# Expert blocks of two half blocks, each with its own expert, in the MoE loop of a two-layer backbone

## What is computed

```python
scores = jax.nn.sigmoid((h @ router_w).astype(jnp.float32))
...
_, idx = lax.top_k(jnp.where(expert_mask, biased, -jnp.inf), TOP_K)     # 8 of 64
...
# assignments sorted by expert, each expert's rows padded to blocks
def run_block(args):
    tok, wt, e = args
    xb = h[tok]
    hid = jax.nn.silu(xb @ w_gate[e]) * (xb @ w_up[e])                  # 1024 -> 256
    return (hid @ w_down[e]) * wt[:, None]                              # 256 -> 1024
```

## Time and profile before

| | |
|---|---|
| time, median of 3 runs | 2135.89 us (2134.73 to 2139.37) |
| the profiled execution | 2138.5 us, its span from first to last instruction 2136.7 us |
| mean granted TensorE clock | 0.948 of full speed |
| busy: TensorE matmul, weight load | 1835.1 us (86%), 992.2 us |
| busy: VectorE, ScalarE, GpSimd | 846.2, 542.0, 426.2 us |
| `up` (L1208) | 5120 matmuls, 643.0 us busy |
| `down` (L1221) | 1264 matmuls, 306.5 us busy |
| expert weights | 384 transfers of 1 MB |
| moved by DMA | 578.28 MB |

### The profile page before, as it was taken

How to read it: one execution, slowest core, us unless ns; L and a number is a source line. 1 busy time by engine, 2 the same in 40 slices (tenths; PEclk the granted TensorE clock), 3 DMA queues, 4 the chain that set the end, 5 groups by cost and what they waited for, 6 DMA issues and landing times. The chain is left out here.

```text
span 2136.7 us, 39465 instructions
## 1 busy us (share of the span) xinstructions
PE 1835.1 (86%) x11495; PEld 992.2 (46%) x11496; DVE 846.2 (40%) x2836; ACT 542.0 (25%) x1163; POOL 426.2 (20%) x417
## 2 busy tenths in 40 slices
PE   4999699879999999999997589879688887888885
PEld 3545454435445545445553355545444444444442
DVE  2245563363333333333334526543532323223334
ACT  2142352222222222222221214233222222222221
POOL 0001300012223223222321000130122222222220
PEclk8999899999999999999999889969799999999998
DMA  8315510449999789897985853631599999999994
GB/s 278 126 66 201 188 60 1 177 170 377 369 388 357 257 309 359 315 376 270 383 334 198 297 158 110 250 129 34 209 354 370 409 399 411 397 406 400 363 385 185
DMA packets 170400, 578.28 MB, mean 271 GB/s; under 512 B 29756, under 2 KB 34592, under 8 KB 153448
## 3 DMA queue, kind: packets, MB, share of 16 engines
q1 hardware_dynamic: 134592, 515.49, 62.7%
q0 software_dynamic: 29056, 60.07, 7.7%
q10 hardware_dynamic: 6696, 1.98, 0.4%
HBM read 565.73 MB, written 45.75 MB: 286 GB/s over the span
## 5 line engine op out<-in xcount | busy, mean ns | idle before, releaser
L1208 PE MATMUL bank<-arena 128*64 128x256 f32 x5120 | 643.0, 395 | 124.8 <-DMA arena<-in_exp_w_down 81.5
L1208 PEld LDWEIGHTS bank<-arena 128*64 128x64 f32 x5120 | 353.0, 140 | 293.1 <-DMA arena<-in_exp_w_down 86.8
L676 POOL DMA_INDIRECT yrows<-arena x158 | 160.3, 1014 | 832.8 <-ACT arena L907 814.7
L1221 PE MATMUL bank<-arena 128*64 128x512 f32 x1264 | 306.5, 606 | 0.7 <-issue 0.5
L657 POOL DMA_INDIRECT arena<-hrows,arena x164 | 185.9, 1133 | 144.3 <-DVE arena L1650 91.6
L1680 DVE TENSOR_TENSOR arena<-arena,bank 64x256 f32<-64x256 f32 x160 | 68.0, 425 | 353.9 <-ACT arena L891 353.8
L902 ACT ACTIVATE arena<-bank 128x128 f32<-128x128 f32 x158 | 44.2, 280 | 565.6 <-PE bank L1227 565.6
L907 ACT ACTIVATE arena<-bank 128x512 f32<-128x512 f32 x158 | 94.4, 597 | 210.1 <-PE bank L1221 210.1
L973 PE MATMUL bank<-arena 128*128 128x512 f32 (+3 forms) x384 | 133.9, 512 | 11.7 <-DVE arena L1337 11.7
L1645 DVE COPY arena<-bank 128x3 f32<-128x3 f32 x164 | 26.4, 161 | 288.9 <-PE bank L1192 288.3
L1199 PE MATMUL bank<-arena 128*128 128x128 f32 x648 | 121.9, 311 | 7.8 <-DMA arena<-hrows,arena 7.8
(11 more groups left out here) (297 smaller groups left out, 1834.1 us busy)
## 6 DMA issues: line engine op xcount, KB each, us to landing
arena<-in_exp_w_gate SPq DMA_DIRECT2D x128, 1024.0 KB, 8.8
arena<-in_exp_w_up SPq DMA_DIRECT2D x128, 1024.0 KB, 11.1
arena<-in_exp_w_down SPq DMA_DIRECT2D x128, 1024.0 KB, 9.0
arena<-in_w_ada SPq DMA_DIRECT2D x10, 3072.0 KB, 13.7
arena<-yrows SPq DMA_DIRECT2D x24, 1024.0 KB, 16.3
arena<-in_w_ada SPq DMA_DIRECT2D x8, 2048.0 KB, 9.9
arena<-in_w_in SPq DMA_DIRECT2D x8, 2048.0 KB, 18.8
arena<-in_w_out SPq DMA_DIRECT2D x4, 2048.0 KB, 12.1
```

The costliest lines, as they stand in the source:

```text
L676: pool.indirect_dma_start(out=yrows, out_offset=bass.IndirectOffsetOnAxis(ap=SIXS[u], axis=0), in_=YSB[u], in_offset=None, bounds_check=2 ...
L1208: ins = pe.matmul(bank[b_par][64 * gu:64 * gu + 64, 0:HID], XGT[b_par][:, c, hh, :], wv[:, gu, hh, c, :], start=(c8 == 0), stop=(c8 == 7))
L1221: ins = pe.matmul(bank[2 + b_par][64 * cg:64 * cg + 64, :], HIDT[b_par][:, c, :], wv[:, c, cg * 512:(cg + 1) * 512], start=(c == 0), stop= ...
```

## The change

A block still has 64 slots, but they are two units of 32, each with its own expert. VectorE counts in units (every expert has at least one), and the table holds a unit's expert. `up` and `down` run on four column groups of 32 columns instead of two of 64: gate and up, times two units; two halves of the output, times two units. So each has twice as many matmuls of the same 256 or 512 moving columns. The ring has four slots, the fourth in the region of `H`; the waits for gate and up on one side and for down on the other are separate. `pe.If` now picks by the slot of the first unit (four) and by whether the second unit has the same expert (two), eight copies of each piece of code. `one_hot` copies the two experts' columns of `KV` to a fixed place (`KVP`), so `meta` looks nothing up.

```diff
-MAXB = (T * TOPK + NE * (SLOTS - 1)) // SLOTS
-TABN = 144
+MAXU = (T * TOPK + NE * (UNIT - 1)) // UNIT + 2
+MAXB = MAXU // 2
+TABN = 208
+NSLOT = 4
...
-        ring = [rRING + 6144 * k for k in range(3)]
+        ring = [rRING + 6144 * k for k in range(3)] + [rH]
...
+                    units_up_to = sp.value_load(TABP[0:1, bass.ds(i * NSLOT + u, 1)], min_val=0, max_val=MAXU)
+                    used = sp.snap((units_up_to + 1) // 2)
+                    sp.wait_ge(sp_land[u], i * 32 + (base_land[u] + 32))
+                    sp.wait_ge(sp_dn[u], i * 16 + 16)
...
+                for e in (0, 1, 3, 2):
+                    if e < 3:
+                        sp.wait_ge(*done_of[P_OUT + e])
+                    else:
+                        sp.wait_ge(pe_sh, 4)
+                        sp.wait_ge(pool_hr, 16 * NTS)
                     load_up(e, e)
                     load_down(e, e)
...
                     for t in TS:
-                        ins = pe.matmul(bank[7][:, 0:3], OH[b_par][:, t, :], KV[:, t, bass.ds(e, 1), :].rearrange("p a c -> p (a c)"),
-                                        start=(t == T0), stop=(t == NT - 1))
+                        for un in range(2):
+                            ins = pe.matmul(bank[7][SLOTS * un:SLOTS * un + SLOTS, 0:3], OH[b_par][:, t, un, :], KVP[b_par][:, t, 3 * un:3 * un + 3],
+                                            start=(t == T0), stop=(t == NT - 1))
...
                         for gu in range(2):
-                            ins = pe.matmul(bank[b_par][64 * gu:64 * gu + 64, 0:HID], XGT[b_par][:, c, hh, :], wv[:, gu, hh, c, :],
-                                            start=(c8 == 0), stop=(c8 == 7))
+                            for un in range(2):
+                                r = 64 * gu + UNIT * un
+                                ins = pe.matmul(bank[b_par][r:r + UNIT, 0:HID], XGT[b_par][:, c, un, hh, :], wv[un][:, gu, hh, c, :],
+                                                start=(c8 == 0), stop=(c8 == 7))
...
+                def experts_of(b):
+
+                    e = expert_of(b * 2)
+                    e2 = expert_of(b * 2 + 1)
+                    return e, pe.snap(e % NSLOT), pe.snap(e2 - e)
+
+                def in_slots(slot, step, body):
+
+                    def pair(k):
+                        with pe.If(step == 0):
+                            body((k, k))
+                        with pe.Else():
+                            body((k, (k + 1) % NSLOT))
+
+                    with pe.If(slot == 0):
+                        pair(0)
+                    with pe.Else():
+                        with pe.If(slot == 1):
+                            pair(1)
+                        with pe.Else():
+                            with pe.If(slot == 2):
+                                pair(2)
+                            with pe.Else():
+                                pair(3)
...
-                        meta(1 - u, b + 3, b + 4, b + 3)
-                        slot_now = None if u == 0 else slot
-                        e = expert_of(b + 1)
-                        slot = pe.snap(e % 3)
+                        meta(1 - u, b + 4, b + 3)
+                        now = None if u == 0 else (e, slot, step)
+                        e, slot, step = experts_of(b + 1)
                         pe.wait_ge(a_xe, b + 2)
...
                         turn_tokens(u, i * 16 + 32)
                         if u == 0:
-                            slot_now = pe.snap(expert_of(b) % 3)
+                            now = experts_of(b)
                         pe.wait_ge(a_h, b + 1)
                         pe.wait_ge(a_y, b + 1)
...
-                for m in range(1, NTOK // SLOTS):
-                    link(dve.scalar_tensor_tensor(out=NB, in0=CNT, scalar=float(m * SLOTS), in1=NB, op0=ALU.is_gt, op1=ALU.add))
+                for m in range(1, NTOK // UNIT):
+                    link(dve.scalar_tensor_tensor(out=NB, in0=CNT, scalar=float(m * UNIT), in1=NB, op0=ALU.is_gt, op1=ALU.add))
+                link(dve.tensor_scalar(NB, NB, 1.0, None, ALU.max))
...
                 def one_hot(par, b, chain):
 
-                    e = expert_of(b)
+                    es = [expert_of(b * 2 + un) for un in range(2)]
                     if not (isinstance(b, int) and b == 0):
                         dve.wait_ge(v_oh, b)
-                    chain(dve.tensor_scalar(RR[:, T0:].unsqueeze(2), GG[:, T0:, bass.ds(e, 1)], BASE[:, 0:1], None, ALU.subtract))
+                    for un in range(2):
+                        dve.tensor_copy(KVP[par][:, T0:, 3 * un:3 * un + 3], KV[:, T0:, bass.ds(es[un], 1), :].rearrange("p t a c -> p t (a c)"))
+                        ins = dve.tensor_scalar(RR[:, T0:, un:un + 1], GG[:, T0:, bass.ds(es[un], 1)], BASE[:, 0:1], None, ALU.subtract)
+                    chain(ins)
```

More of the change, by code:

```diff
@@ L235, in build @@
         NBH = at(o, 1); o += 1
-        RR = at(o, 4); o += 4
+        RR = at(o, NT, 2); o += 8
+        KVP = [at16(o + 12 * k, NT, 6) for k in range(2)]; o += 24
+        EB2 = at(o, 2); o += 2
         BASE = at(o, 1); o += 1
@@ L416, in landed @@
             return sp_land[k], 16 * sum(d for m, d in enumerate(dmas_of[:n + 1]) if slot_of(m) == k)
[L418 removed]
+        base_land = [16 * sum(d for m, d in enumerate(dmas_of) if slot_of(m) == k) for k in range(NSLOT)]
         with nc.Block() as block:
@@ L1200, in turn_tokens, with up @@
                     ins.then_inc(pe_x, 1)
-                def up(b_par, k, chunks, last):
-                    wv = at(ring[k], 2, 2, 4, HID)
+                def up(b_par, ks, chunks, last):
+                    wv = [at(ring[k], 2, 2, 4, HID) for k in ks]
                     for c8 in chunks:
@@ new lines, in down_landed, with down @@
+                def down_landed(e, ks):
+                    k, k2 = ks
+                    pe.wait_ge(sp_dn[k], e * 4 + (16 - 4 * k))
+                    if k2 != k:
+                        pe.wait_ge(sp_dn[k2], e * 4 + (20 - 4 * k2))
+                def down(b_par, ks):
+                    wv = [at(ring[k] + 4096, 2, DM) for k in ks]
+                    for c in range(2):
+                        for un in range(2):
+                            for cg in range(2):
+                                r = 64 * un + UNIT * cg
+                                ins = pe.matmul(bank[2 + b_par][r:r + UNIT, :], HIDT[b_par][:, c, UNIT * un:UNIT * un + UNIT],
+                                                wv[un][:, c, cg * 512:(cg + 1) * 512], start=(c == 0), stop=(c == 1))
+                    ins.then_inc(pe_dn, 1)
@@ L1234, in _, with first_up @@
                 turn_tokens(0, 16)
-                meta(0, 2, 3, 2)
+                meta(0, 3, 2)
                 turn_tokens(1, 16)
-                e = expert_of(0)
+                _, _, step = experts_of(0)
                 pe.wait_ge(a_xe, 1)
-                for k in range(3):
-                    with pe.If(e % 3 == k):
-                        expert_landed(e, k)
-                        up(0, k, range(8), True)
+                def first_up(ks):
+                    up_landed(0, ks)
+                    up(0, ks, range(8), True)
+                with pe.If(step == 0):
+                    first_up((0, 0))
+                with pe.Else():
+                    first_up((0, 1))
                 with pe.Fori(0, pairs) as i:
```

120 lines of the change are left out of this document (55 added, 65 removed).

## The result

The changed kernel takes 3977.05 us (median of 4 runs, 3962.26 to 3983.86) beside 2136.37 us of before on the same chip: ratio 1.862, 95% interval 1.857 to 1.866. The profiled execution has a span of 3975.4 us, 1838.7 more than before's 2136.7. The forecast of 3601 us had the sign, the place and the mechanism; it was 376 us short.

A forecast was written before the change was run, and what follows sets the result against it. Before, TensorE paced layer 0 and the weight stream layer 1; changed, reloaded code was to bound both. 2138.5 plus 1005 (layer 0), 458 (layer 1) and 4 gave 3605.5, in terms of the median 3601 us; range 2040 to 4400.

The forecast's parts named there:

- Blocks and array: Expert loops: 80 and 48 blocks; four column groups run side by side, so array time per block stays 4.1, 0.7, 1.9 us.
- sequencer: TensorE's instruction handling, lookups and branches: a pass of two blocks takes 17.9 us in layer 0, even 9.5, odd 8.4.
- Rival 1: All code pieces stay; the sequencer's pass decides layer 0, +31 us: 2173 us (2115 to 2230); chance 0.26.
- Rival 2: Faster: pieces stay and the sequencer keeps up, deciding from 8.4 us a block downwards; about 2050 us; chance 0.12.
- Rival 3: Four groups don't overlap with weights of 32 columns: 14.3 us a block, 2730 us; chance 0.07.
- The store: TensorE's instruction memory: holds at least 4 pieces, upper size unknown; the changed loop's 11.4 pieces likelier don't fit.
- Entries a pass: Expert loops on TensorE: a pass enters, and so loads again, about ten of the body's 11.4 code pieces.
- Price of an entry: Loading a code piece: between 1.5 and 5.9 us, middle 3.7, less 1.3 hidden, so 2.4 us each.
- The parts outside the loops: VectorE's longer tables and one-hots before the loops, +13 us, less 9 for the expert loaded early: +4.
- The weights: Fourth slot and separate `w_down` semaphore load one more expert early: 8.5 us off layer 1's stream, nothing in layer 0.

The follow-up runs named there:

- the run whose code stays: The changed kernel with both halves of a block taking the first expert's weights (one slot's weights), halving the code copies: 2152.0 us beside 2150.8, ratio 1.0004.

## Why the prediction was right, and where it was short

**Blocks and array: right; sequencer: right in the sum.** 80 and 48 blocks; 4.11 us for `up` with its transposes (forecast 4.1), 1.92 for `down` (1.9), both at the full clock; 17.35 us a pass with code that stays (17.9 with four choices more), one interval 8.0 and the other 9.4 (8.4, by its own terms 8.5, and 9.5). That the pass came out so well is partly luck, for its steps were off in both directions. The sequencer leaves the longer `up` 3.1 us after its start in the block shown (714.51 to 717.64) and 3.7 in the median of layer 0, not 2.5, and is 24 instructions ahead in that block, not 38, so the earlier trace rows was no fixed lead. Against that, in the pass around 725 us two lookups take 1.6 us (1.8 in the forecast), `down` starts 5.5 us after its `up` (6.1), and the next `up` 3.0 after `down` (3.4). Rival 1, all pieces stay, gave 2173 us, 34 more than before, with 2115 to 2230 around it: the run whose code stays takes 2152 beside 2151, within that range. It failed at its condition alone. Rival 2's point, 8.4 us a block, was just not reached (8.68, on a chip whose own point is 687.3 / 80 = 8.6). Rival 3 is excluded by the 4.11 us.

**The store: right as a choice, open as a size.** The rows of the forecast gave four pieces as the lower bound and nothing above. It is seven for a loop, so 11.4 were out of reach, and by a wide margin.

**Entries a pass: too few.** I took about ten of 11.4; the trace has 12, for the body lies across twelve pieces (16.8 to 27.9) and the pieces at its ends count whole. At 2.4 us that is 40 x 1.9 x 2.4 = 182 us in layer 0 and 24 x 2.0 x 2.4 = 115 in layer 1, the largest of the terms that were mis-sized.

**Price of an entry: right for layer 0, low for layer 1.** Layer 0: (46.2 - 17.35) / 11.9 = 2.42 us, with 2.4 forecast; from the run that only moves a loop, 2.36. Layer 1: (50.9 - 17.4) / 12.0 = 2.79, which makes 24 x 12 x 0.39 = 112 us. Part of that is the weight traffic (a DMA share of 0.58 in layer 1's window, 0.34 in layer 0's; quarter transfers take 5.3 us off its pass and 3.7 off layer 0's); the rest is open. That 2.4 itself was met is partly luck: it is the middle of 1.5 and 5.9, less 1.3 that I took as hidden, and the same sum missed the unrolled loops, at 0.9. How it is made up I had wrong as well: by the estimate above some 0.3 of it is the lower clock, for which the working had nothing.

**The sum.** Layer 0: 40 x 46.2 = 1848 for 1680 (+168: entries 182, price 10, the shorter chain -22); layer 1: 24 x 50.9 = 1222 for 1008 (+214: 115, 112 and -12). The parts outside the loops were to bring +4 and brought 31: 11 ahead of the first `down` of layer 0 and 20 between the loops. That is where VectorE's longer tables and one-hots lie, and the first entries into the new code; the run with one slot's weights has 12 and 5 there, so some 15 of the 31 go with the larger code. I didn't trace them further. These terms add up to 409 us, and the span was 372 longer than forecast. The rest is the way of counting: the forecast took 40 and 24 whole passes, but from first `down` to last there are 39.5 and 23.5 (21 and 25 us less), and its 550 us of before begin at `up`, 11 us ahead of the first `down`.

**The weights: right in size, wrong in effect.** The fourth slot was to give 8.5 us in layer 1; alone it gives 13, in the changed kernel nothing to be seen, since the stream no longer bounds it. The forecast says as much of the stream and takes the 8.5 us off its sum all the same; they don't belong there. That the slot costs layer 0 16 us through the tests was in none of my terms.

## What to carry to other kernels

Count the instructions between a loop's head and its closing branch before anything else, copies for each case included, whether they run or not: on TensorE a loop that lay in 7 pieces of 256 ran from its store, one that lay in 8 paid 2.4 us for every piece in every turn (0.9 where the loop was unrolled and more of each piece was run through), and the same 1,669 instructions cost 961 us more or nothing depending on where they began. Cases written out as copies multiply (four slots by one or two experts by two parities made 11 pieces of 2.4), and the queue of instruction fetches in the profile, divided by the turns of the loop, tells at once. A deeper buffer is worth its extra test only in the stage that the stream bounds: here 13 us gained in one layer and 16 lost in the other.

## What the runs showed of the hardware that I had not expected

A loop too long for the store is fetched whole in each turn, not by its excess: 8.2 pieces a turn for a body of 7.1, 10.8 for one of 9.5. Code that is only jumped over is fetched all the same (797 pieces more for copies that never run). A stall of the sequencer has an echo in the clock: with 20 us of lookups a pass and no fetch in the loops the granted clock went from 0.99 to 0.71 and 48 products from 2.80 to 5.21 us. And a test that is never true costs its row and a little more: some 6.7 of them a pass (1.67 a choice, four choices) made it 1.7 us longer beside the kernel unrolled twice, 0.25 each, where the rows of branches say 0.07 to 0.22.
